# Lag, block sums and reload buffers of the second norm in a conv/pool decoder layer on eight cores

## Chip, cores and metric

The kernel runs on the 8 cores of one Trainium2 chip. Each core takes one of the 8 prompt sequences (2048 tokens) and 16 of the 128 sample sequences (128 tokens), with its own copy of the weights, and no core talks to another. The metric is the device time of the slowest core, in microseconds (us); lower is better. TensorE (matmul) is called PE here, VectorE is DVE, ScalarE is ACT, GpSimd is POOL, and SyncE (which issues most DMAs) is SP.

## What is computed

```python
h = rmsnorm(x, g_pre_mix)
p = h @ w_in                        # xv | b | c | u | gates
ya, conv_new = short_gated_conv(xv, bg, cg, conv_buf, w_conv)
ya = ya @ w_out_conv
yb, pool_new = multiscale_pool(u, pool_buf, start_pos, w_pool_group, pool_scale)
merged = gates[..., :D_MODEL] * ya + gates[..., D_MODEL:] * yb
x = x + rmsnorm(merged @ w_o, g_post_mix)
h2 = rmsnorm(x, g_pre_mlp)
f = jnp.square(jax.nn.relu(h2 @ w_up)) @ w_down
x = x + rmsnorm(f, g_post_mlp)
```

D_MODEL is 1024, D_FF is 4096, and x is float32. The matmuls run in bfloat16.

## The kernel before

A core has 17 tiles of 128 tokens: tiles 0 to 7 are half 0 of the sequence, tiles 8 to 15 half 1, and tile 16 holds the sample tokens. One big SBUF array, `AR`, is laid out by hand in byte offsets, so that buffers of later stages lie where those of earlier stages have ended. The helper class `Prog` keeps one list of instructions for each engine in the order in which the program calls them, finds dependences by overlapping bytes, and turns them into semaphore waits. An engine therefore runs its own list strictly in order, and a wait holds up all that stands behind it on that engine. The work is a list `steps`; `at_step(s, ...)` puts weight loads (issued by POOL) ahead of step s.

**Mixer.** Phase A (`a_unit`) makes the convolution branch, phase B (`phase_b`: `u_unit`, `m_unit`) the pooling branch and the gates, for half 0 and then for half 1 with the sample tokens. `phase_b(1)` ends at step `n_b`. Its last six steps are the units `m_unit` of channel blocks 6 and 7, and have no pooling work.

**Mixer tiles.** Each tile goes through three functions. `s_mm(i)` is 16 matmuls with w_o into one of four pairs of PSUM banks. `s_b1(i)` is the first norm: ACT squares and sums the pair (`sq_mix`), takes a square root, DVE takes the reciprocal and writes the scaled product (`mixn`, which frees the banks), and POOL adds the residual x in place (`x1`). `s_b2(i)` is the second norm: SP stores x1 to HBM (`x1store`), ACT squares it (`sq_x1`) and takes the root, DVE takes the reciprocal and writes `hn`, SP reloads the raw x of tile i + 3 (`load_xr`) into the buffer just left, and SP issues a DMA transpose of `hn` into the token columns of the MLP's input. Tiles 0 to 7 are spread over phase A of half 1. Tiles 8 to 16 run as one block of nine steps (`tiles2`), in the order `s_mm(i)`, `s_b2(i - 1)`, `s_b1(i)`, with three residual buffers in turn.

**MLP.** Each half is one level of a Strassen-Winograd scheme. `h_sums` makes four sums of quarters of the tokens' matrix (DVE, 128x2048 bfloat16 each), and `up_sums` four sums of weight blocks for one of 8 column blocks (DVE, 128x1024 each). `up_step(half, p)` has seven groups of 8 matmuls, three for column block p - 1 (`up_old` parts 6, 7, 4) and four for block p (`up_new` parts 1, 5, 2, 3), with DVE and ACT work between them, and calls `up_sums` for block p + 1. Half 1 also has the sample tokens in each step (`up_sample`). In half 0, step 0, `s_b2(16)` and `up_sums(0, 0)` stand ahead of all the rest. The down projection is `d0` to `d6`. `d5` and `d6` finish the output tiles: they need x1 again (`load_xl`), which goes through two buffers (`XL`). Tile t's buffer is used again for tile t + 2, whose load is issued once tile t has left it. In `d6` each tile has `gp0`, a reciprocal (L1256) and two `yl` on DVE, and two output stores on SP. Half 1 follows half 0 at once.

L139, L143, L156, L159, L169 are the lines in `Prog`'s helpers for matmul, transpose on PE, activation, tensor_tensor and scalar_tensor_tensor, so the rows are told apart by shape and time. L129 is the helper for DMAs.

Of the kernel before, what the change touches and what calls it, by code (L numbers as in the profile page):

```python
# [300 lines left out]
def build_program():  # L301
# [41 lines left out]
    with stack:  # L343
# [120 lines left out]
        XR_.append([arv(76992 + i * 4096, F32, [D]) for i in range(3)])  # L464
# [314 lines left out]
        def s_buf(i):  # L779
            v = 0 if i < 8 else 1  # L780
            return (XR_[v][i % 3], arv(MT_[v][i % 2], F32, [D]), arv(MT_[v][i % 2], BF16, [D]),
                    HN_[v][i % len(HN_[v])])

        def load_xr(i):
            P.dma("sp", s_buf(i)[0], xsrc(i), "xr%d" % (i % 3), name="xreload")
# [25 lines left out]
        def s_b2(i):  # L811
            x1, mt, mtj, hn = s_buf(i)
            x1_store[i] = P.dma("sp", x1_d[i, :, :], x1, "x1s%d" % (i % 3), name="x1store")
# [4 lines left out]
            if i + 3 < NT and (i >= 8 or i + 3 < 8):  # L818
                load_xr(i + 3)
# [33 lines left out]

        def b_last():
# [28 lines left out]
        XL = [arv(4096 + i * 4096, F32, [D]) for i in range(2)]  # L883
# [19 lines left out]
        def h_sums(half):  # L903
            t1, t2, t3, t4 = (ts_at(half, i) for i in range(4))
            P.tt("dve", t1, hq(half, 1), hq(half, 0), ALU.subtract, name="hs")
            P.tt("dve", t2, hq(half, 3), t1, ALU.subtract, name="hs")
            P.tt("dve", t3, hq(half, 3), hq(half, 1), ALU.subtract, name="hs")
            P.tt("dve", t4, hq(half, 2), t2, ALU.subtract, name="hs")
# [126 lines left out]
        def up_step(half, p, extra=()):  # L1035
# [97 lines left out]
        def d0(half):  # L1133
# [4 lines left out]
            for i in (0, 1) if half == 0 else (SMP, 9):  # L1138
                load_xl(i)
# [43 lines left out]
        def d3(half):  # L1183
# [17 lines left out]
            if half == 1:  # L1201
# [41 lines left out]
        def d6(half):  # L1243
            tl = HT[half]
            for i in range(4):
# [3 lines left out]
                xl = XL[t % 2]  # L1249
# [10 lines left out]
                if i < 2:  # L1260
                    load_xl(tl[6 + i])
# [167 lines left out]
```

How the kernel before makes its waits and increments, by code:

```python
    def emit(self, stack):  # L180
# [33 lines left out]
                            continue  # L214
                        key = d.eng
                        val = d.wait_val
                        assert val is not None, (d.name, op.name)
                    if waited.get(key, 0) >= val:
                        continue
                    if need.get(key, 0) < val:
                        need[key] = val
                for key, val in need.items():
                    waited[key] = val
                    eng.wait_ge(sems[key], val)
                    nwait += 1
                if op.fn is not None:
                    ins = op.fn(eng)
                    if op.dma is not None:
                        ins.then_inc(sems[("dma", op.dma[0])], 16)
                    elif op.signal:
                        ins.then_inc(sems[e], 1)
        return nwait
```

## Time and profile before

| | before |
|---|---|
| median of 3 runs | 1017.28 us (1015.13 to 1017.82) |
| the profiled execution | 1024.65 us |
| its span on the slowest core, core 6 | 1023.6 us |
| spans of the other cores | 1008.0 to 1019.2 us |
| mean granted clock of core 6, cores 0 to 7 | 0.958; 0.953 to 0.966 |
| PE busy | 941.8 us (92%) |
| DVE busy | 638.2 us (62%) |
| ACT busy | 361.0 us (35%) |
| POOL busy | 200.1 us (20%) |

The profiled execution was 7.4 us above the median of the runs. Times in rows are microseconds from the first instruction of core 6's span. A timeline row has start, duration, engine, line, operation and operands (output<-input), shapes and count, and in brackets the engine's idle time before it and what ended it; a row of several instructions gives the time from the first start to the last end. The duration of an instruction is from its start to its end, waits inside it included. PEclk is the share of full clock that the throttle granted.

### The profile page before, as it was taken

The page shows a single profiled execution, that of the slowest core. Times are in us where ns is not written, and L with a number is a line of the kernel's source. Part 1 is how long each engine was busy: PE and PEld are TensorE (multiplying, and loading weights), DVE is VectorE, ACT ScalarE, POOL GpSimd, SP SyncE. Part 2 cuts the span into 40 slices and gives each one's busy share as a digit, 9 for nine tenths or more (in the row PEclk, how much of TensorE's full clock was granted, in tenths as well). Part 3 has the DMA queues.
Part 4 walks back from the last instruction along what each step waited for, and adds up shares of the span by engine and source line. Part 5 has one row for each costly group of instructions (what it writes and reads, how often), then busy time and mean ns, then how long its engine had stood idle before and what let it go on. Part 6 is the DMA issues. An engine that isn't in the chain of part 4 may idle for free.

```text
span 1023.6 us, 15629 instructions; the slowest of 8 cores (1008.0 to 1023.6 us)
## 1 busy us (share of the span) xinstructions
PE 941.8 (92%) x5078; PEld 456.8 (45%) x5078; DVE 638.2 (62%) x960; ACT 361.0 (35%) x723; POOL 200.1 (20%) x203
## 2 busy tenths in 40 slices
PE   6899999999999999999961699999997899999996
PEld 4554444444455455455420244444443355544442
DVE  2567766763766666776336677658374767556186
ACT  2343432322444443233333455520133455520222
POOL 5520000000122110000133124230021243240021
PEclk7999999999999999999996799889998899999999
DMA  9699953523667653312386747594347539068027
GB/s 180 158 251 180 182 115 62 89 43 75 148 137 140 124 84 52 63 33 109 68 196 178 124 81 122 86 194 75 55 133 204 117 69 163 4 113 134 1 74 255
DMA packets 50575, 119.48 MB, mean 117 GB/s; under 512 B 21952, under 2 KB 22208, under 8 KB 50240
## 3 DMA queue, kind: packets, MB, share of 16 engines
q0 software_dynamic: 17712, 65.54, 39.6%
q1 hardware_dynamic: 32496, 52.64, 17.3%
q8 instruction: 43, 0.70, 0.3%
q14 instruction: 36, 0.29, 0.1%
q10 hardware_dynamic: 288, 0.30, 0.1%
HBM read 160.53 MB, written 19.01 MB: 175 GB/s over the span
## 4 chain that ended last, share of the span: by engine, by line
PE 72%; DVE 9%; DMA 6%; issue 5%; POOL 4%; ACT 4%; DVEq 0%; SPq 0%; ACTq 0%; POOLq 0%
PE PS L139 72%; DVE AR L169 4%; DVE AR L159 4%; ACT AR L156 3%; DMA AR<-x_d 3%; POOL AR L159 3%; DMA AR<-x_p 2%; DMA AR<-w_a 1%; DMA AR<-w_o 1%; POOL AR L164 1%; DVE STAT L427 1%; ACT STAT L156 0%; PE PS L143 0%; DVEq L224 0%; DVE AR L164 0%
## 5 line engine op out<-in xcount | busy, mean ns | idle before, releaser
L139 PE MATMUL PS<-AR 128*128 128x512 bf16 (+1 forms) x4920 | 927.0, 352 | 56.0 <-DVE AR L159 34.3
L139 PEld LDWEIGHTS PS<-AR 128*128 128x128 bf16 x4920 | 445.6, 100 | 532.2 <-issue 102.8
L156 ACT ACTIVATE AR<-PS 128x512 f32<-128x512 f32 (+3 forms) x266 | 158.6, 601 | 357.2 <-PE PS L139 315.4
L159 DVE TENSOR_TENSOR AR<-AR 128x1024 bf16<-128x1024 bf16 (+10 forms) x268 | 236.8, 903 | 70.9 <-PE PS L139 28.8
L159 DVE TENSOR_TENSOR AR<-PS,AR 128x512 f32<-128x512 f32 (+1 forms) x249 | 159.4, 649 | 154.6 <-PE PS L139 142.8
L159 POOL TENSOR_TENSOR AR<-AR 128x512 bf16<-128x512 f32 (+1 forms) x66 | 113.4, 1726 | 436.5 <-DVE AR L169 254.5
L156 ACT ACTIVATE AR<-AR 128x1024 bf16<-128x1024 f32 (+3 forms) x131 | 95.3, 739 | 115.2 <-DVE AR L159 54.7
L169 DVE SCALAR_TENSOR_TENSOR AR<-AR,CS 128x512 f32<-128x512 f32 (+1 forms) x80 | 58.3, 729 | 40.0 <-ACT AR L156 20.0
L156 ACT ACTIVATE AR<-PS,CS 128x512 f32<-128x512 f32 (+1 forms) x80 | 48.9, 621 | 76.8 <-PE PS L139 69.1
L169 DVE SCALAR_TENSOR_TENSOR AR<-AR 128x512 bf16<-128x512 f32 (+4 forms) x100 | 60.4, 629 | 3.9
L156 ACT ACTIVATE AR<-AR,CS 128x512 f32<-128x512 f32 (+1 forms) x40 | 26.3, 658 | 94.3 <-DVE AR L159 94.3
L169 DVE SCALAR_TENSOR_TENSOR AR<-AR,STAT 128x1024 bf16<-128x1024 f32 (+2 forms) x42 | 46.3, 1119 | 20.1 <-DMA AR<-x_d 16.4
L427 DVE RECIPROCAL STAT<-STAT 128x1 f32<-128x1 f32 x60 | 9.5, 158 | 65.1 <-ACT STAT L156 64.7
L129 POOL DMA_DIRECT2D AR<-w_up x32 | 17.7, 556 | 99.5 <-PE PS L139 99.2
L129 POOL DMA_DIRECT2D AR<-w_m x16 | 8.7, 544 | 139.3 <-PE PS L139 139.1
L129 POOL DMA_DIRECT2D AR<-w_a x32 | 17.6, 571 | 63.4 <-PE PS L139 57.8
L159 DVE TENSOR_TENSOR AR<-PS,CS 128x1024 bf16<-128x1024 bf16 x17 | 20.7, 1217 | 14.5 <-PE PS L143 14.5
L169 DVE SCALAR_TENSOR_TENSOR AR<-PS,CS,AR 128x512 f32<-128x512 f32 (+1 forms) x40 | 26.4, 661 | 0.0
L143 PE MATMUL PS<-IDB,AR 128*128 128x128 bf16 x136 | 11.6, 235 | 13.7 <-POOL AR L164 11.5
L169 DVE SCALAR_TENSOR_TENSOR AR<-PS,STAT,AR 128x1024 f32<-128x1024 f32 x17 | 21.8, 1284 | 2.2 <-DVE STAT L427 0.9
L164 POOL TENSOR_SCALAR AR<-AR,STAT 128x1024 bf16<-128x1024 f32 x7 | 19.9, 2848 | 15.8 <-ACT AR L156 10.6
L156 ACT ACTIVATE STAT<-STAT,CS 128x1 f32<-128x1 f32 x60 | 17.7, 294 | 5.7 <-ACT AR L156 0.4
(36 smaller groups left out, 96.4 us busy)
## 6 DMA issues: line engine op xcount, KB each, us to landing
AR<-x_p SPq DMA_DIRECT2D x32, 512.0 KB, 8.4
AR<-w_dn POOLq DMA_DIRECT2D x32, 512.0 KB, 16.0
AR<-w_m POOLq DMA_DIRECT2D x16, 768.0 KB, 10.0
AR<-w_up POOLq DMA_DIRECT2D x16, 768.0 KB, 8.9
x_d<-AR SPq DMA_DIRECT2D x17, 512.0 KB, 3.4
AR<-x_d SPq DMA_DIRECT2D x17, 512.0 KB, 4.9
AR<-w_a POOLq DMA_DIRECT2D x24, 256.0 KB, 11.0
AR<-w_a POOLq DMA_DIRECT2D x8, 768.0 KB, 9.4
```

The source lines that it names most:

```text
L129: op = self.add(q, lambda e: e.dma_start(out=out, in_=in_, **kw), reads=[in_], writes=[out], name=name, dma=(semkey, cnt))
L139: return self.add("pe", lambda e: e.matmul(out, lhsT, rhs, start=start, stop=stop, **kw), reads=[lhsT, rhs], writes=[out], signal=sig, nam ...
L143: return self.add("pe", lambda e: e.transpose(out, in_, ident), reads=[in_, ident], writes=[out], signal=signal, name="tr")
L156: return self.add("act", lambda e: e.activation(out, in_, func, **kw), reads=rd, writes=wr, name=name)
L159: return self.add(eng, lambda e: e.tensor_tensor(out, in0, in1, op), reads=[in0, in1], writes=[out], name=name)
L164: return self.add(eng, lambda e: e.tensor_scalar(out, in0, s1, s2, op0), reads=rd, writes=[out], name=name)
L169: return self.add(eng, lambda e: e.scalar_tensor_tensor(out, in0, scalar, in1, op0, op1), reads=rd, writes=[out], name=name)
L427: P.add("dve", lambda e: e.reciprocal(ss, ss), reads=[ss], writes=[ss], name="rstd")
```

## The change

The reloads of x for tiles 8 to 16 get six buffers in place of three. Those of tiles 8 to 12 are issued seven steps ahead of the end of phase B (with the state outputs, `b_last`), that of tile 13 at the first tile's step, and tile i + 6 follows in `s_b2(i)`. In `tiles2` the order becomes `s_mm(i)`, `s_b1(i)`, `s_b2(i - 2)`; `s_b2(15)` and `s_b2(16)` go into half 0's first up step, between its groups of matmuls. The four `h_sums(0)` go behind four of the last six steps of phase B, one each. `up_sums(0, 0)` goes behind the step of tile 14. Two weight loads (`load_up`) are issued a step or two sooner. x1 of each output tile has a place of its own in `AR` or one that is long free, and is loaded at the start of `d0`, `d4` and `d5`. Two pieces of `load_dn(0, 2)` and three of `load_dn(1, 1)` are issued sooner.

```diff
-        XR_.append([arv(76992 + i * 4096, F32, [D]) for i in range(3)])
+        XR_.append([arv(b_, F32, [D]) for b_ in (143360, 147456, 76992, 81088, 85184, 55296)])
...
-            if i + 3 < NT and (i >= 8 or i + 3 < 8):
-                load_xr(i + 3)
+            nx = i + 3 if i < 8 else i + 6
+            if (i < 8 and nx < 8) or (i >= 8 and nx < NT):
+                load_xr(nx)
...
+        def after(s, fn):
+            f = steps[s]["f"]
+            steps[s]["f"] = lambda: (f(), fn())
+
+        def b_tail():
+            b_last()
+            for t in range(8, 13):
+                load_xr(t)
+        after(n_b - 7, b_tail)
...
-        XL = [arv(4096 + i * 4096, F32, [D]) for i in range(2)]
+        XLB = dict(enumerate((4096, 8192, 12288, 43008, 47104, 75776, 79872, 38912,
+                              8192, 43008, 47104, 75776, 79872, 34816, 38912, 67584, 4096)))
...
+        for n_, d_ in enumerate((6, 5, 3, 2)):
+            after(n_b - d_, lambda n_=n_: h_sums(0, [n_]))
...
-        def up_step(half, p, extra=()):
+        def up_step(half, p, extra=(), mid=()):
+            mid = list(mid)
...
+            if mid:
+                mid.pop(0)()
...
-            for i in (0, 1) if half == 0 else (SMP, 9):
-                load_xl(i)
+            load_xl(*((0, 1, 2) if half == 0 else (SMP, 8)))
...
         def d4(half):
+            load_xl(*((3, 4, 5, 6) if half == 0 else (9, 10, 11, 12)))
...
         def d5(half):
             tl = HT[half]
+            load_xl(*((7,) if half == 0 else (13, 14, 15)))
...
-                out_tile(half, i, t1v(half, i), XL[t % 2], ydst(t))
-                load_xl(tl[i + 2])
+                out_tile(half, i, t1v(half, i), xl_at(t), ydst(t))
...
-                if i < 2:
-                    load_xl(tl[6 + i])
...
                 if n_ == 0:
-                    b_last()
-                    for t in range(8, 11):
-                        load_xr(t)
+                    load_xr(13)
                 s_mm(i)
-                if n_ > 0:
-                    s_b2(i - 1)
                 s_b1(i)
+                if n_ > 1:
+                    s_b2(i - 2)
                 if n_ == 6:
-                    h_sums(0)
+                    up_sums(0, 0)
             step(O_KEYS, fn)
-        at_step(n_b, lambda: load_up(0, 0))
-        at_step(n_b + 2, lambda: load_up(0, 1))
+        at_step(n_b - 2, lambda: load_up(0, 0))
+        at_step(n_b + 1, lambda: load_up(0, 1))
...
-                    if half == 0 and p == 0:
-                        s_b2(NT - 1)
-                        up_sums(0, 0)
                     if p == 8:
-                        up_step(half, p, [lambda pc=pc: d_p1(half, pc) for pc in range(4)])
+                        up_step(half, p, [lambda pc=pc: d_p1(half, pc) for pc in range(4)],
+                                [lambda: None, lambda: load_dn(1, 1, (0, 1, 2))] if half == 1 else ())
+                    elif half == 0 and p == 0:
+                        up_step(half, p, mid=[lambda: s_b2(NT - 2), lambda: s_b2(NT - 1)])
```

## Rows read from the trace of the kernel before

**Rows 1.** Who waited for whom, engine PE, whole span: total, times, longest us
```profile
PE PS L139 <- DVE AR L159: 34.3, 4, 27.4
PE PS L139 <- DVE AR L169: 12.6, 4, 3.7
```
**Rows 2.** Timeline of PE, the rows that begin after an idle time
```profile
572.23 208.38 PE L139 MATMUL PS<-AR 128*128 128x512 bf16 x920 [27.35 <-DVE AR L159]
787.24 6.04 PE L139 MATMUL PS<-AR 128*128 128x128 bf16 x44 [6.62 <-DVE STAT L1256]
...
937.71 76.13 PE L139 MATMUL PS<-AR 128*128 128x512 bf16 x352 [2.23 <-DVE AR L159]
```
**Rows 3.** Busy time by stretch, core 6: PE, PEld, DVE, ACT, POOL, PEclk, DMA share, GB/s
```profile
499.00:516.00 17.00, 17.00 (x80) 7.64 (x78) 4.57 (x8) 7.47 (x14) 5.75 (x4) 1.00 0.40 107
...
570.00:575.00 5.00, 2.77 (x7) 1.05 (x8) 4.62 (x8) 0.60 (x1) 0.00 (x0) 0.50 0.97 129
585.00:590.00 5.00, 5.00 (x21) 2.14 (x20) 4.79 (x8) 2.88 (x6) 2.02 (x2) 0.84 0.42 80
```
**Rows 4.** Timelines of ACT, DVE and POOL around tiles 8 to 10 of the block
```profile
499.12 1.02 ACT L156 ACTIVATE AR<-PS 128x1024 bf16<-128x1024 f32 x1 [3.70 <-PE PS L139]
503.95 2.34 POOL L159 TENSOR_TENSOR AR<-AR 128x1024 f32<-128x1024 f32 x1 [19.50 <-DVE AR L169]
506.38 1.06 ACT L156 ACTIVATE AR<-AR 128x1024 bf16<-128x1024 f32 x1 [4.48 <-POOL AR L159]
508.43 1.28 DVE L169 SCALAR_TENSOR_TENSOR AR<-AR,STAT 128x1024 bf16<-128x1024 f32 x1 [0.24 <-DVE STAT L427]
509.93 1.28 DVE L169 SCALAR_TENSOR_TENSOR AR<-PS,STAT,AR 128x1024 f32<-128x1024 f32 x1
511.42 2.36 POOL L159 TENSOR_TENSOR AR<-AR 128x1024 f32<-128x1024 f32 x1 [5.13 <-DVE AR L169]
```
**Rows 5.** Timelines of DVE and POOL where instructions of both meet
```profile
268.88 2.35 POOL L159 TENSOR_TENSOR AR<-AR 128x1024 f32<-128x1024 f32 x1 [11.31 <-DVE AR L169]
269.04 0.69 DVE L159 TENSOR_TENSOR AR<-PS,AR 128x512 f32<-128x512 f32 x1 [0.31 <-PE PS L139]
547.86 6.76 DVE L159 TENSOR_TENSOR AR<-AR 128x2048 bf16<-128x2048 bf16 x4
548.15 3.12 POOL L159 TENSOR_TENSOR AR<-AR 128x1024 f32<-128x1024 f32 x1 [5.00 <-DVE AR L169]
992.13 2.35 POOL L159 TENSOR_TENSOR AR<-AR 128x1024 f32<-128x1024 f32 x1 [4.78 <-DMA AR<-x_d]
993.28 2.27 DVE L169 SCALAR_TENSOR_TENSOR AR<-AR,STAT 128x1024 f32<-128x1024 f32 x1
```
**Rows 6.** DMA issues, 480 to 620 us: count, KB each, median us to landing
```profile
AR<-w_up POOLq DMA_DIRECT2D x7, 768.0 KB, 8.9
```
**Rows 7.** Timeline of DVE: one set of `up_sums`, beside no POOL add
```profile
586.21 3.53 DVE L159 TENSOR_TENSOR AR<-AR 128x1024 bf16<-128x1024 bf16 x4
```
**Rows 8.** Who waited for whom, engine DVE, whole span
```profile
DVE AR L169 <- DMA AR<-x_d: 16.4, 6, 8.9
DVE AR L159 <- DMA AR<-w_dn: 9.6, 4, 2.8
```
**Rows 9.** Timeline of DVE, end of half 0's `d6`
```profile
784.97 1.42 DVE L169 SCALAR_TENSOR_TENSOR AR<-AR,STAT 128x512 f32<-128x512 f32 x2 [8.95 <-DMA AR<-x_d]
787.91 1.41 DVE L169 SCALAR_TENSOR_TENSOR AR<-AR,STAT 128x512 f32<-128x512 f32 x2 [0.86 <-DMA AR<-x_d]
791.91 2.05 DVE L169 SCALAR_TENSOR_TENSOR AR<-AR,STAT 128x512 f32<-128x512 f32 x2 [1.91 <-DMA AR<-x_d]
```
**Rows 10.** Timelines of ACT and DVE, the last output tile
```profile
1013.94 0.60 ACT L156 ACTIVATE AR<-PS 128x512 bf16<-128x512 f32 x1 [2.38 <-PE PS L139]
1019.80 1.42 DVE L169 SCALAR_TENSOR_TENSOR AR<-AR,STAT 128x512 f32<-128x512 f32 x2 [1.71 <-DMA AR<-x_d]
```
**Rows 11.** Busy time by stretch, core 6, mixer part of half 1
```profile
260.00:500.00 240.00, 240.00 (x1440) 122.20 (x1439) 159.40 (x283) 92.59 (x212) 25.20 (x23) 1.00 0.48 97
```

More of the change, by code:

```diff
@@ L780, in s_buf @@
             v = 0 if i < 8 else 1
-            return (XR_[v][i % 3], arv(MT_[v][i % 2], F32, [D]), arv(MT_[v][i % 2], BF16, [D]),
+            return (XR_[v][i % 3 if i < 8 else (i - 8) % 6], arv(MT_[v][i % 2], F32, [D]), arv(MT_[v][i % 2], BF16, [D]),
                     HN_[v][i % len(HN_[v])])
         def load_xr(i):
-            P.dma("sp", s_buf(i)[0], xsrc(i), "xr%d" % (i % 3), name="xreload")
+            P.dma("sp", s_buf(i)[0], xsrc(i), "xr%d" % (i % 6), name="xreload")
         s_bank = {}
@@ L812, in s_b2 @@
             x1, mt, mtj, hn = s_buf(i)
-            x1_store[i] = P.dma("sp", x1_d[i, :, :], x1, "x1s%d" % (i % 3), name="x1store")
+            x1_store[i] = P.dma("sp", x1_d[i, :, :], x1, "x1s%d" % (i % 6), name="x1store")
             ss = stat()
@@ L901, in build_program, with h_sums @@
         T_1, T_2, T_3, T_4 = range(4)
-        def h_sums(half):
+        def h_sums(half, which=range(4)):
             t1, t2, t3, t4 = (ts_at(half, i) for i in range(4))
[L905 to L908, printed above, removed]
+            for o_, a_, b_ in [((t1, hq(half, 1), hq(half, 0)), (t2, hq(half, 3), t1),
+                                (t3, hq(half, 3), hq(half, 1)), (t4, hq(half, 2), t2))[i] for i in which]:
+                P.tt("dve", o_, a_, b_, ALU.subtract, name="hs")
+        for n_, d_ in enumerate((6, 5, 3, 2)):
+            after(n_b - d_, lambda n_=n_: h_sums(0, [n_]))
         def up_raw(half, b, i):
@@ L1051, in up_step @@
                 fill.pop(0)()
+            if mid:
+                mid.pop(0)()
             if o is not None:
@@ L1077, in load_dn, with xl_at, load_xl @@
                 P.dma("pool", bq(half, q, 4 * pc, 4), w_dn[q, pc], "dn%d_%d" % (q, pc), name="wload")
-        def load_xl(i):
-            P.dma("sp", XL[i % 2], x1_d[i, :, :], "xl%d" % (i % 2), name="x1load", deps=[x1_store[i]])
+        def xl_at(i):
+            return arv(XLB[i], F32, [D])
+        def load_xl(*ts):
+            for i in ts:
+                P.dma("sp", xl_at(i), x1_d[i, :, :], "xl%d" % (i % 8 if i < 16 else 8), name="x1load", deps=[x1_store[i]])
         def d_mm(bk, lhs, i, rhs, us, start, stop, sig):
@@ L1212, in d3 @@
                 b_sum(half, 2, 2, 0, ALU.subtract)
-                out_tile(half, 0, SMT, XL[0], ydst(SMP))
-                load_xl(HT[half][0])
+                out_tile(half, 0, SMT, xl_at(SMP), ydst(SMP))
         def d4(half):
+            load_xl(*((3, 4, 5, 6) if half == 0 else (9, 10, 11, 12)))
             for pc in range(4):
@@ L1248, in d6 @@
                 t = tl[4 + i]
-                xl = XL[t % 2]
+                xl = xl_at(t)
                 s0, s1 = dn[("s0", i)], stat()
@@ L1295, in build_program @@
                         at_step(s_, lambda: load_dn(0, 0))
+                    if p == 6:
+                        at_step(s_, lambda: load_dn(0, 2, (0, 1)))
                     if p == 7:
-                        at_step(s_, lambda: load_dn(0, 2))
+                        at_step(s_, lambda: load_dn(0, 2, (2, 3)))
                     if p == 8:
@@ L1313, in build_program @@
                     else:
-                        at_step(s_, lambda: (load_dn(1, 1), load_dn(1, 3)))
+                        at_step(s_, lambda: (load_dn(1, 1, (3,)), load_dn(1, 3)))
                 if n_ == 4 and half == 0:
```

## The prediction

> **What bounds the kernel now.** I read the waits of PE first, because PE is busy 941.8 of 1023.6 us. PE loses 34.3 us to DVE tensor_tensors, 27.4 of it at one point, and 12.6 us in four waits of about one tile each [rows 1]. The timeline of PE places them. It stands from 544.9 to 572.23, then 6.62 us ahead of 787.24 (and 4.75 more by 800) and 2.23 ahead of 937.71 [rows 2]. So three places are worth looking at, and the end of the program is a fourth.
>
> At the first place, the block of tiles 8 to 16, the products are not what takes time. ACT starts on tile 8's pair at 499.12 [rows 4], and 80 matmuls (five tiles) fill 499 to 516.2 without a gap [rows 3], so a tile's product is 3.44 us. Nine tiles need 31 us, yet the up projection goes on only at 572.23. One cycle shows why: POOL adds x1 for 2.34 us, then ACT squares it (506.38, 1.06 us), then DVE writes `hn` (508.43) and only behind it `mixn` of the next tile (509.93), which the next POOL add waits for (511.42) [rows 4]. From 503.95 to 511.42 is 7.5 us, and it repeats. Work of two tiles is strung into one chain, because `s_b2(i - 1)` stands ahead of `s_b1(i)` on ACT and DVE.
>
> **Part A, the lag of two tiles.** With `s_b1(i)` first and `s_b2(i - 2)` behind, nothing waits for POOL's last add. Each engine's own load per tile is then PE 3.44, ACT about 3.1 (from 506.38 to 508.43 there is a square, its root and DVE's reciprocal; 1.55 of it is ACT's, twice a tile), DVE 2.9 (two of 1.28 and two reciprocals), POOL 2.35. PE would set the pace, but for one thing. `hn` reads two operands in the SBUF, and so does POOL's add, and until now they never ran together. Where such a pair does meet, they take turns. The add from 992.13 to 994.48 left the DVE instruction of 993.28 at 2.27 us instead of 1.28, and at 547.86 POOL's add took 3.12 and four `h_sums` 6.76. A DVE instruction with one operand in the PSUM ran inside an add at its plain 0.69 (269.04) [rows 5]. So `hn` and the add are taken in turn, 1.2 + 2.35 = 3.55 us a tile, a little over PE's 3.44.
>
> Order of time, worked from 499.0:
> - PE: tile 16's product ends at 499.0 + 8 x 3.44 = 526.5.
> - POOL: x1(8) ends at 506.3; the two issues of `load_up(0, 1)`, now ahead of x1(9), take 1.1; x1(9) ends at 509.8. Then five turns of 3.55: x1(14) ends at 527.5.
> - `up_sums(0, 0)`, 3.53 us [rows 7], two-operand too, to 531.1. Then `mixn`, `hn` and x1 of tile 15 to 536.3, and those of tile 16 to 540.0.
> - The rest of tile 16 stands ahead of the next sums: ACT 1.5, DVE's `hn` 1.5, `up_sums(0, 1)` 3.5, two `C11` and two `rsq` 2.6, the first `C12` 0.7. It ends at 549.8, and PE, which has run ahead to `up_old` part 7 of step 1 with short stops, waits for it. Five groups of 8 matmuls (1.72 each) end step 1 at 558.4. Coming out of several us of stops the clock is down to 1.2 GHz for a while, as now at 570 to 575 (0.50) [rows 3]; I add 1.5: 560.
>
> Before, PE had 80 matmuls (17.2 us) left from 572.23 to the end of step 1, lost 1.4 us at 0.50 and 1.2 at 0.84 [rows 3], and ended it at 592. **Part A: 32 us less.** Bounds: if all meetings cost nothing, x1(16) ends 5 us sooner, 37; if POOL wins each meeting (rival 1), 21.
>
> What else moves here is covered. Four `h_sums` (6.76 us now, with an add taking its turn, so some 4.8 alone) go to the last six units of phase B, where DVE is under half loaded and PE has two sets of banks: nothing, and 1 to 2 us if a unit's banks were late. The reloads of tiles 14 to 16 wait on SP for the store of the tile whose buffer they take: SP has a store, a reload and a transpose per tile, and even at 8.9 us for a landing [rows 6], the longest of this stretch's kinds, x(14) issued at 511 is there by 520 and needed at 525. `load_up(0, 2)` stands behind x1(16) on POOL, is issued at 541 and lands by 550; `up_sums(0, 2)` wants it at 554. This cover is 4 us thin (rival 2).
>
> **Part B, x1 at the end of half 0.** DVE waits 16.4 us in all for x1 reloads [rows 8], and 8.95 + 0.86 + 1.91 = 11.7 of it here [rows 9]: two buffers, each reload behind the tile that frees it. The new loads of tiles 3 to 7 are issued 25 to 40 us ahead of use, into bytes whose last reader (`d3` or `d4`) is done by then. With the waits gone DVE's next limit is its own work, which has no gap there; PE's stop of 6.62 and most of the later one go. PE's clock, lowered by these stops, gives back 1.3, an estimate from the 1.4 at 0.50 in part A. **13 us less**, between 10 and 15. The six buffers cost SP nothing: the same count of loads, sooner.
>
> **Part C, three pieces of `load_dn(1, 1)` sooner.** DVE waits 9.6 us for w_dn pieces [rows 8], `C11` stands behind them on DVE and holds the banks for `d2`: PE's 2.23 [rows 2]. The pieces now go ahead of POOL's two squares and start about 6 us sooner. **2.2 less**, between 0 and 2.2.
>
> **Part D, the end.** DVE's other waits for x1, 4.6 us, lie in half 1's last tiles. ACT starts on the last product at 1013.94 (PE is done), and the last `yl` ends at 1021.2 [rows 10]. Without waits the end is 1013.9 + 1.1 for ACT (0.60, its read and root) + 0.3 for the reciprocal + 1.5 for two `yl` = 1017.0. **4.2 less**, between 2 and 4.5.
>
> **Sum.** 32 + 13 + 2.2 + 4.2 = 51.4. The profiled execution goes from 1024.65 to 973.2. It was 7.4 above the median of the runs; from the median, 1017.28 - 51.4 = 965.9, and I say 966.
>
> **Rivals.**
> 1. *POOL wins every meeting.* `mixn` starts, and POOL's add starts 1.49 us after it (509.93, 511.42); `hn` would start some 1.47 after it. If POOL is first, `hn` waits 2.35 and holds up the next `mixn`: 5.2 us a tile. For: the two starts are within 0.1. Against: from x1(9), which is late by the 1.1 us of DMA issues, `hn` is already waiting when an add ends, and then keeps first place. It costs 1.6 x 7 = 11 us: 977. By the Trainium skill, SBUF — State Buffer, section "Who interferes with whom", whoever issued first holds the port for the whole instruction; that says the same of a meeting, and not who is first here.
> 2. *Weights late.* Stores, transposes and reloads of nine tiles now share some 45 us with two `load_up`. If `load_up(0, 2)` lands 4 to 9 us beyond 550, PE waits up to 5: 971. For: a share of 0.84 to 1.0 is reached now when they meet. Against: five reloads have moved ahead of the block.
> 3. *Slower: the clock.* With the gaps gone, eight cores run dense at once. Stretches granted 0.84 and less stand in the trace now [rows 3]. From 592 to the last matmul at 1013.8, less 13.5 us of stops, PE has 408 us of work; at 0.81 it costs 94 us more, 1060, and from 220 us of it on the gain of 51 is gone. For: such stretches came behind the gap. Against: the same cores ran 240 of 240 us dense at a granted 1.00 in the mixer [rows 11]. The Trainium skill (TensorE: Matmul & The Clock Gate, section "Seeing it yourself") has a limit that takes a die to 13/16 of full clock once three of its cores run dense, while the load lasts; by it the whole rest would be at that clock and the change would lose. Rows 11 speak against it as a standing state.
> 4. *The reload waits stay*, because SP is held by some wait ahead of the new loads: 966 + 17 = 983. I see none: what stands ahead of them are stores of tiles done by then.
> 5. *Better.* No meeting costs anything, and the stretch at 0.84 behind the gap goes too: 966 - 5 - 5 = 956.
>
> **Chances.** Forecast, to within 6 us, 0.62; rival 1 0.13; rival 2 0.08; rival 3 0.03; rival 4 0.04; rival 5 0.10. The low bound takes rival 5 and the best of parts B and D: 952. The high one takes rival 1 with 6 us of a thin part B or of more clock loss: 983. About 0.3% (3 us) is what a measurement can tell. Faster 0.95, same 0.02, slower 0.03.
>
> **What would show it.** Right: POOL's adds of tiles 10 to 16 3.5 to 3.7 us apart; `hn` often 1.5 to 2.5 us long; tile 16's product ended near 527; one stop of PE of 5 to 7 us ahead of step 1's part 7; step 1 over near 560; no wait of DVE for x1; no PE stop at 787 and 937; 3.3 us from the last matmul to the last `yl`. Wrong: adds 5 us apart (rival 1), a DVE wait for w_up (rival 2), granted clock below 0.9 over a hundred us (rival 3), or DVE waits on x1 (rival 4).

## The result, and the profile after

| | before | after |
|---|---|---|
| median | 1017.55 us, 4 runs (1015.13 to 1019.12) | 971.78 us, 4 runs (971.48 to 972.59) |
| ratio | | 0.9553, 95% interval 0.9533 to 0.9573 |
| the profiled execution | 1024.65 us | 972.59 us |
| its span on the slowest core | 1023.6 us, core 6 | 971.5 us, core 3 |
| spans of the other cores | 1008.0 to 1019.2 us | 961.8 to 967.7 us |
| mean granted clock, cores 0 to 7 | 0.953 to 0.966 | 0.980 to 0.989 |
| PE busy | 941.8 us (92%) | 932.3 us (96%) |
| DVE busy | 638.2 us (62%) | 644.5 us (66%) |
| ACT busy | 361.0 us (35%) | 360.5 us (37%) |
| POOL busy | 200.1 us (20%) | 202.4 us (21%) |

The kernel is 45.8 us faster; 51.4 were forecast. Core 6 was the slowest before and core 3 is now, so the two traces are compared on core 3, whose span went from 1015.4 to 971.5 us. A few executions of the kernels below ran in a slower state, with cores of one die at a lower granted clock; all medians here leave them out, while two expectations name a median that did not (984.8 for 984.1).

The timeline of PE of the kernel after, core 3, the rows that begin after an idle time; [rows 2] is the same view of before:

```profile
533.70 6.38 PE L139 MATMUL PS<-AR 128*128 128x512 bf16 x16 [4.16 <-DVE AR L159]
541.58 5.34 PE L139 MATMUL PS<-AR 128*128 128x512 bf16 x24 [1.50 <-ACT AR L156]
553.95 197.35 PE L139 MATMUL PS<-AR 128*128 128x512 bf16 x924 [7.03 <-DVE AR L159]
752.50 1.02 PE L139 MATMUL PS<-AR 128*128 128x512 bf16 x4 [1.20 <-DVE AR L159]
754.89 210.92 PE L139 MATMUL PS<-AR 128*128 128x512 bf16 x1136 [1.38 <-DVE AR L159]
```

The same view of the kernel before, now of core 3:

```profile
519.25 3.61 PE L139 MATMUL PS<-AR 128*128 128x512 bf16 x16 [2.56 <-DVE AR L169]
533.85 5.30 PE L139 MATMUL PS<-AR 128*128 128x512 bf16 x16 [3.68 <-DVE AR L169]
...
572.84 201.10 PE L139 MATMUL PS<-AR 128*128 128x512 bf16 x920 [27.42 <-DVE AR L159]
778.34 7.32 PE L139 MATMUL PS<-AR 128*128 128x128 bf16 x44 [4.41 <-DVE STAT L1256]
788.72 1.02 PE L139 MATMUL PS<-AR 128*128 128x512 bf16 x4 [3.06 <-DVE AR L159]
791.12 135.12 PE L139 MATMUL PS<-AR 128*128 128x512 bf16 x784 [1.38 <-DVE AR L159]
928.00 76.13 PE L139 MATMUL PS<-AR 128*128 128x512 bf16 x352 [1.75 <-DVE AR L159]
```

The stop of 27.42 us, and four of 2.56 to 3.69 ahead of it (two are shown, 12.7 together), have become stops of 4.16, 1.50 and 7.03. Those of 4.41 and 3.06 have become one of 1.20, and that of 1.75 is gone. The row of four matmuls (1.02 us) is the same work in both, so the two can be laid side by side there. At it the kernel after is 788.72 - 752.50 = 36.2 us ahead. Part B's stops are 4.41 + 3.06 - 1.20 = 6.3 of it, which leaves 29.9: 27.4 for part A's stops (27.42 + 12.7 - 12.69) and 2.5 for the clock behind the stops of both parts. The last matmul ends at 1004.13 before and at 965.81 after, 38.3 ahead: 2.1 for part C (its stop was 1.75). The spans differ by 43.9: 5.6 for part D.

The granted clock was not the same on all cores before. Busy time by stretch in the kernel before, cores 6 and 3:

```profile
640.00:655.00 15.00, 15.00 (x59) 6.26 (x58) 10.85 (x16) 7.08 (x12) 3.55 (x4) 0.81 0.43 76
```

```profile
640.00:655.00 15.00, 15.00 (x71) 6.82 (x70) 12.24 (x20) 8.05 (x14) 5.42 (x7) 1.00 0.35 60
```

All eight cores have 0.81 to 0.85 from 585 to 590. Only cores 4 to 7 have it again from 640 to 655, and cores 6 and 7 once more from 670 to 685. The same 920 matmuls took 208.38 us on core 6 [rows 2] and 201.10 on core 3. In the profiled execution of the kernel after, no core has such a stretch from 560 to 960 us, but for core 3 behind its stop ahead of 752.50.

Who waited for whom, DVE and then PE of the kernel after, core 3, whole span (total, times, longest us). In the whole view for DVE there is no row for x_d, where core 3 of before has 16.0 us in six waits and core 6 had 16.4 [rows 8]:

```profile
DVE AR L159 <- DMA AR<-w_dn: 6.2, 3, 2.3
...
PE PS L139 <- DVE AR L159: 14.2, 5, 7.0
```

The block of tiles 8 to 16 in the kernel after, core 3, timelines of ACT, of POOL and then of DVE:

```profile
500.34 1.02 ACT L156 ACTIVATE AR<-PS 128x1024 bf16<-128x1024 f32 x1 [3.70 <-PE PS L139]
...
508.68 4.75 POOL L159 TENSOR_TENSOR AR<-AR 128x1024 f32<-128x1024 f32 x2
516.12 2.41 POOL L159 TENSOR_TENSOR AR<-AR 128x1024 f32<-128x1024 f32 x1 [2.69 <-DVE STAT L427]
521.46 6.58 POOL L159 TENSOR_TENSOR AR<-AR 128x1024 f32<-128x1024 f32 x2 [2.94 <-ACT AR L156]
528.61 2.35 POOL L159 TENSOR_TENSOR AR<-AR 128x1024 f32<-128x1024 f32 x1 [0.56 <-DVE STAT L427]
541.59 2.34 POOL L159 TENSOR_TENSOR AR<-AR 128x1024 f32<-128x1024 f32 x1 [2.75 <-DVE STAT L427]
...
516.15 3.47 DVE L169 SCALAR_TENSOR_TENSOR AR<-AR,STAT 128x1024 bf16<-128x1024 f32 x1
521.25 1.28 DVE L169 SCALAR_TENSOR_TENSOR AR<-AR,STAT 128x1024 bf16<-128x1024 f32 x1
528.64 3.40 DVE L169 SCALAR_TENSOR_TENSOR AR<-AR,STAT 128x1024 bf16<-128x1024 f32 x1
541.56 3.45 DVE L169 SCALAR_TENSOR_TENSOR AR<-AR,STAT 128x1024 bf16<-128x1024 f32 x1
```

The chain of [rows 4] is broken: x1(9) starts at 508.68 and x1(14) at 528.61, which is 4.0 us a tile, where it was 7.5. x1(16) ends at 543.9. The four `hn` shown are either 1.28 or 3.4 to 3.5 us long. Five of the block's nine are long, one took 1.66 and three 1.28, and it is the same five on all eight cores. All `hn` of the program stand together in a view of instructions grouped by shape (busy us, mean ns), here of the kernel before and then of the kernel after:

```profile
L169 DVE SCALAR_TENSOR_TENSOR AR<-AR,STAT 128x1024 bf16<-128x1024 f32 x17 | 21.8, 1284 | 2.5 <-DVE STAT L427 1.5
```

```profile
L169 DVE SCALAR_TENSOR_TENSOR AR<-AR,STAT 128x1024 bf16<-128x1024 f32 x17 | 33.0, 1938 | 2.5 <-DVE STAT L427 1.5
```

It is the same work at 11.2 us more: time in which DVE stands beside POOL's adds.

The end of the kernel after, timelines of PE, ACT and DVE, which answers to [rows 10]:

```profile
963.71 2.11 PE L139 MATMUL PS<-AR 128*128 128x512 bf16 x9
965.91 0.60 ACT L156 ACTIVATE AR<-PS 128x512 bf16<-128x512 f32 x1 [2.38 <-PE PS L139]
967.57 1.41 DVE L169 SCALAR_TENSOR_TENSOR AR<-AR,STAT 128x512 f32<-128x512 f32 x2
```

From the last matmul (965.8) to the end of the last `yl` (968.98) is 3.2 us.

### The profile page after: what moved, and what is told of

Same layout as the page of the kernel before. It is cut to its first block, busy times and chain, and to the rows that moved or that the text cites. A ratio compares the mean times of both kernels' runs of the same rounds, so it can differ in the third digit from the quotient of the medians.

```text
span 971.5 us, 15639 instructions; the slowest of 8 cores (961.8 to 971.5 us)
## 1 busy us (share of the span) xinstructions
PE 932.3 (96%) x5078; PEld 453.1 (47%) x5078; DVE 644.5 (66%) x960; ACT 360.5 (37%) x723; POOL 202.4 (21%) x203
## 4 chain that ended last, share of the span: by engine, by line
PE 82%; DVE 7%; issue 5%; POOL 2%; DMA 2%; ACT 2%; DVEq 0%; ACTq 0%; POOLq 0%
PE PS L139 81%; DVE AR L159 3%; DVE AR L169 3%; ACT AR L156 1%; DMA AR<-w_o 1%; POOL AR L164 1%; DMA AR<-x_p 1%; POOL AR L159 1%; POOL AR L129 0%; PE PS L143 0%; DVEq L224 0%; DVE STAT L427 0%; DVE AR L164 0%; ACT L156 0%; DVE FAC L498 0%
## 5 line engine op out<-in xcount | busy, mean ns | idle before, releaser
L139 PE MATMUL PS<-AR 128*128 128x512 bf16 (+1 forms) x4920 | 916.6, 349 | 20.1 <-DVE AR L159 14.2
L169 DVE SCALAR_TENSOR_TENSOR AR<-AR,STAT 128x1024 bf16<-128x1024 f32 (+2 forms) x42 | 55.8, 1345 | 5.0 <-DVE STAT L427 2.2
L129 POOL DMA_DIRECT2D AR<-w_up x32 | 17.8, 560 | 89.8 <-PE PS L139 89.5
L129 POOL DMA_DIRECT2D AR<-w_a x32 | 17.9, 584 | 63.9 <-PE PS L139 57.8
L159 DVE TENSOR_TENSOR AR<-PS,CS 128x1024 bf16<-128x1024 bf16 x17 | 20.7, 1219 | 13.3 <-PE PS L143 13.3
L164 POOL TENSOR_SCALAR AR<-AR,STAT 128x1024 bf16<-128x1024 f32 x7 | 19.9, 2849 | 12.9 <-DVE STAT L427 12.7
L143 PE MATMUL PS<-IDB,AR 128*128 128x128 bf16 x136 | 11.6, 234 | 11.2 <-POOL AR L164 9.2
```

The costliest lines, as they stand in the source:

```text
L129: op = self.add(q, lambda e: e.dma_start(out=out, in_=in_, **kw), reads=[in_], writes=[out], name=name, dma=(semkey, cnt))
L139: return self.add("pe", lambda e: e.matmul(out, lhsT, rhs, start=start, stop=stop, **kw), reads=[lhsT, rhs], writes=[out], signal=sig, nam ...
L143: return self.add("pe", lambda e: e.transpose(out, in_, ident), reads=[in_, ident], writes=[out], signal=signal, name="tr")
L159: return self.add(eng, lambda e: e.tensor_tensor(out, in0, in1, op), reads=[in0, in1], writes=[out], name=name)
L164: return self.add(eng, lambda e: e.tensor_scalar(out, in0, s1, s2, op0), reads=rd, writes=[out], name=name)
L169: return self.add(eng, lambda e: e.scalar_tensor_tensor(out, in0, scalar, in1, op0, op1), reads=rd, writes=[out], name=name)
```

## The experiments

Each changes the kernel after. The kernel before was run beside them, in three groups, with medians of 1019.0, 1017.1 and 1019.6 us; beside the kernel after it had 1017.55. A difference is therefore given by the medians and, in brackets, by the ratios (difference of the ratios x 1017.55). The intervals of the ratios are 2 to 7 us wide on each side, so differences below about 3 us are not told apart by times.

**A lag of one tile, the other parts kept.**

```diff
                 s_mm(i)
+                if n_ > 0:
+                    s_b2(i - 1)
                 s_b1(i)
-                if n_ > 1:
-                    s_b2(i - 2)
...
-                        up_step(half, p, mid=[lambda: s_b2(NT - 2), lambda: s_b2(NT - 1)])
+                        up_step(half, p, mid=[lambda: s_b2(NT - 1)])
```

> The changed kernel with the second norm one tile behind the first again, and ahead of it (s_b2(i - 1), then s_b1(i)); all else stays. Theory (the lag is what breaks the chain of POOL's add, the second square, hn, mixn): the adds stand 7.3 us apart again, x1 of tile 16 ends near 562 to 566, the first C12 some 20 us later than in the changed kernel, and the time is 992, 988 to 997. Rival (the sooner sums and the six reload buffers took most of the block's gain, the order little): under 980.

Measured: 991.42 us, ratio 0.9729 (0.9712 to 0.9746), 19.6 us more than the kernel after (17.9). POOL's timeline of this kernel, two adds in the block:

```profile
511.14 2.34 POOL L159 TENSOR_TENSOR AR<-AR 128x1024 f32<-128x1024 f32 x1 [3.97 <-DVE AR L169]
518.36 2.35 POOL L159 TENSOR_TENSOR AR<-AR 128x1024 f32<-128x1024 f32 x1 [4.89 <-DVE AR L169]
```

The adds are 7.2 us apart again, so the chain of [rows 4] is what the order of `s_b1` and `s_b2` makes, and nothing else of the change breaks it.

**The token and weight sums late, the lag kept.**

```diff
-        for n_, d_ in enumerate((6, 5, 3, 2)):
-            after(n_b - d_, lambda n_=n_: h_sums(0, [n_]))
...
                 if n_ == 6:
-                    up_sums(0, 0)
+                    h_sums(0)
...
+                        up_sums(0, 0)
```

> The changed kernel with the four h_sums behind tile 14's step again and the first up_sums at the start of the up projection. Theory (both then stand on DVE ahead of the first products that PE can't do without, and h_sums also delay the norms of tiles 15 and 16): 6 to 10 us slower, 978 to 982. Rival (the lag leaves DVE room for them): within 2 us of the changed kernel, 970 to 974.

Measured: 980.76 us, ratio 0.9624 (0.9605 to 0.9643), 9.0 us more (7.2). PE's timeline of this kernel:

```profile
550.47 10.79 PE L139 MATMUL PS<-AR 128*128 128x512 bf16 x40 [22.68 <-DVE AR L159]
```

PE cannot run ahead into the up steps, because their sums come last on DVE. With the lag alone a stop of 22.68 us would still stand there.

**Two x1 buffers at the end, the rest kept.** `XL` has two buffers in turn again, and tile t + 2 is loaded once tile t has left its buffer.

```diff
-            return arv(XLB[i], F32, [D])
+            return arv(4096 + (i % 2) * 4096, F32, [D])
...
                 out_tile(half, i, t1v(half, i), xl_at(t), ydst(t))
+                load_xl(tl[i + 2])
```

> The changed kernel with two x1 buffers for the output tiles again, each load issued as before behind the tile that frees its buffer. Theory (parts B and D of the forecast): DVE waits 16 us again for x1, 12 of it at the end of half 0 and 4 to 5 at the end of the program, and the time is 983 to 989. Rival (only the waits at the end of the program reach the time, those of half 0 are caught up by PE): 975 to 978.

Measured: 986.72 us, ratio 0.9682 (0.9665 to 0.9699), 14.9 us more (13.1). Waits of DVE over the whole span, and PE's timeline:

```profile
DVE AR L169 <- DMA AR<-x_d: 15.3, 6, 5.3
...
748.53 6.20 PE L139 MATMUL PS<-AR 128*128 128x128 bf16 x44 [2.97 <-DVE STAT L1278]
758.95 1.07 PE L139 MATMUL PS<-AR 128*128 128x512 bf16 x4 [4.22 <-DVE AR L159]
```

The waits of [rows 8] are back, six of them as before, and with them PE's two stops.

**`load_dn(1, 1)` whole in `d0` again.**

```diff
-                        up_step(half, p, [lambda pc=pc: d_p1(half, pc) for pc in range(4)],
-                                [lambda: None, lambda: load_dn(1, 1, (0, 1, 2))] if half == 1 else ())
+                        up_step(half, p, [lambda pc=pc: d_p1(half, pc) for pc in range(4)])
...
-                        at_step(s_, lambda: (load_dn(1, 1, (3,)), load_dn(1, 3)))
+                        at_step(s_, lambda: (load_dn(1, 1), load_dn(1, 3)))
```

> The changed kernel with all four pieces of load_dn(1, 1) issued in d0 again. Theory (part C of the forecast): PE stops about 2 us ahead of half 1's d2, and the time is 973.5 to 974.5. Rival (no core waits there any more, since the slowest cores differ): 971 to 972.5.

Measured: 974.22 us, ratio 0.9553 (0.9496 to 0.961), 2.4 us more by the medians and nothing by the ratios. The time alone says nothing here; PE's timeline does:

```profile
891.92 76.13 PE L139 MATMUL PS<-AR 128*128 128x512 bf16 x352 [2.13 <-DVE AR L159]
```

The stop ahead of these 352 matmuls, 2.23 in [rows 2], is back on the core shown. The 2.4 us are not this stop alone: in the same execution all eight cores had 0.81 to 0.86 of the clock from 565 to 570 us, cores 4 to 7 until 580, which the profiled execution of the kernel after does not show and this edit, in half 1, cannot reach.

**Three reload buffers with the lag.**

```diff
-        XR_.append([arv(b_, F32, [D]) for b_ in (143360, 147456, 76992, 81088, 85184, 55296)])
+        XR_.append([arv(b_, F32, [D]) for b_ in (143360, 147456, 76992)])
...
-            nx = i + 3 if i < 8 else i + 6
+            nx = i + 3
```

> The changed kernel with three reload buffers for tiles 8 to 16: tiles 8 to 10 loaded ahead, tile i + 3 in s_b2(i). Theory (a loop of three tiles: hn 1.3, landing 4.4 to 6, add 2.35, square and root 1.5, hn, so 3.5 to 4.5 us a tile, which is less than the 5.1 that a blocked hn makes of it): small, 972 to 977, and POOL waits for x_p. Rival (the reloads, now behind hn of the tile two back, set the pace of the block): 982 to 990.

Measured: 992.44 us, ratio 0.9728 (0.9666 to 0.9791), 20.7 us more (17.8). That is above the range of the rival, whose mechanism it is. Waits of POOL, from 480 to 620 us:

```profile
POOL AR L159 <- DMA AR<-x_p: 21.4, 5, 5.3
```

With three buffers the reload of tile i + 3 stands behind the second norm of tile i, which now comes two tiles later, and five of the adds wait for their residual. The kernel before, with three buffers and a lag of one, has no such wait on any core. So the six buffers would save nothing there, yet all that the lag gives hangs on them.

**`hn` with one operand in the SBUF.** The weight row `g_pre_mlp` is copied into a pair of PSUM banks that is held for the block. The products and the first up steps have three pairs left.

```diff
+                    gp.append(bank2())
+                    held.update((gp[0], gp[0] + 1))
+                    P.copy("act", pair(gp[0]), GPL, name="gpl")
...
-            P.stt("dve", hn, x1, ss, GPL, ALU.mult, ALU.mult, name="hn")
+            if gp:
+                P.stt("dve", hn, pair(gp[0]), ss, x1, ALU.mult, ALU.mult, name="hn")
+            else:
+                P.stt("dve", hn, x1, ss, GPL, ALU.mult, ALU.mult, name="hn")
```

> The changed kernel with g_pre_mlp copied once by ACT into a pair of PSUM banks held for the block of tiles 8 to 16, so that hn has one operand in the SBUF and POOL's add has no partner to take turns with; the products then have three pairs of banks. Theory (hn and the add exclude each other while both read two operands in the SBUF): each hn of the block takes 1.28 us, none 3.4; the adds follow the products 3.5 us apart; x1 of tile 16 ends 6 to 10 us sooner, and the time is 964, 961 to 967. Rival (the long hn are hidden by PE's lead of four tiles or made up later): 970 to 973. A third (three pairs of banks hold PE up): above 973.

Measured: 984.14 us, ratio 0.9664 (0.9639 to 0.9688), 12.4 us *more* (11.3). The spans of the profiled execution fall into two groups: cores 0, 1, 3, 6 and 7 took 955.1 to 963.6 us, less than any core of the kernel after but core 6, and cores 2, 4 and 5 took 973.3 to 979.5. Core 3 is of the first group. Its `hn` of this block grouped by shape, POOL's adds of tiles 12 to 14 and 16, and PE's last stop:

```profile
L169 DVE SCALAR_TENSOR_TENSOR AR<-PS,STAT,AR 128x1024 bf16<-128x1024 f32 x9 | 11.6, 1283 | 1.1 <-DVE STAT L427 0.4
...
515.81 2.36 POOL L159 TENSOR_TENSOR AR<-AR 128x1024 f32<-128x1024 f32 x1 [0.79 <-DVE STAT L427]
519.11 2.36 POOL L159 TENSOR_TENSOR AR<-AR 128x1024 f32<-128x1024 f32 x1 [0.93 <-DVE STAT L427]
522.56 2.35 POOL L159 TENSOR_TENSOR AR<-AR 128x1024 f32<-128x1024 f32 x1 [1.09 <-DVE STAT L427]
532.51 2.35 POOL L159 TENSOR_TENSOR AR<-AR 128x1024 f32<-128x1024 f32 x1 [0.70 <-DVE AR L169]
...
545.87 74.37 PE L139 MATMUL PS<-AR 128*128 128x512 bf16 x336 [3.80 <-DVE AR L159]
```

No `hn` is stretched, the adds of tiles 12 to 14 are 3.3 to 3.5 us apart, and PE's last stop ends at 545.87 in place of 553.95. (Its block began 1.9 us sooner; the other 6.2 are the gain.) That much came as expected. The time lies where the third theory, too few banks, would have it, but that is not the cause: with the same three pairs and no transposes, further down, this kernel took 963.54. Core 2 is of the other group; its stretch, one transpose on SP's queue, and the DMA view from 480 to 620 us (count, KB each, median us to landing):

```profile
530.00:550.00 20.00, 14.96 (x69) 6.33 (x68) 11.66 (x18) 11.02 (x21) 5.72 (x9) 1.00 1.17 111
...
532.90 18.87 SPq L828 DMA_TRANSPOSE AR<-AR  x1
...
AR<-w_up POOLq DMA_DIRECT2D x7, 768.0 KB, 28.4
```

The packets' times add up to 1.17 of what the DMA engines have, and they move only 111 GB/s (the jam, from here on); on core 3 the same 20 us show 1.07 at 238 GB/s. One transpose keeps SP for 18.87 us and weights land after 28.4 us in place of 8.1 on core 3. There DVE waits 27.0 us for w_up. Late weights alone do not mark a slow core, though: they landed after 17.3 and 14.4 us on cores 1 and 6 of the fast group, and after 10.4 and 9.5 on cores 4 and 5. Nor does one transpose of 10 us, which cores 0, 1 and 3 have too (10.2 to 10.9). Core 4 shows another wait (ACT's waits from 480 to 620 us, then PE's timeline):

```profile
ACT AR L156 <- DMA AR<-AR: 25.7, 4, 17.9
...
561.15 3.57 PE L139 MATMUL PS<-AR 128*128 128x512 bf16 x8 [18.08 <-DVE AR L169]
```

ACT's `sq_x1` writes an `hn` buffer whose transpose is still under way (it keeps SP for 18.71 us), and PE stands for 18.08 us behind it.

**The jam: which transfers?** Two tries first moved work out of its way. In one, `load_up(0, 2)` is issued with tile 12's step, ahead of POOL's later adds:

```diff
+        at_step(n_b + 4, lambda: load_up(0, 2))
```

> The kernel of the run e3_hn_psum, with load_up(0, 2) issued three steps sooner, ahead of tile 12's add and not behind tile 16's. In that run six cores took 955 to 964 us, and one to three others 973 to 985, where stores, transposes and two load_up issued back to back met and some landed 20 to 39 us late. Theory (the two loads together behind the last add, on top of five transposes in flight, make the jam): no core with a landing of w_up or a transpose over 20 us behind 530, the slowest core at 962 to 966. Rival (any load beside the denser stores and transposes can jam): again one or more cores 10 us and more above the others, 975 to 985.

Measured: 984.91 us, ratio 0.9665 (0.9598 to 0.9731), no better. Core 5, the slowest, by stretch:

```profile
540.00:550.00 10.00, 5.04 (x16) 1.83 (x16) 1.45 (x2) 1.59 (x5) 0.00 (x0) 0.83 1.35 50
```

The other also has `up_sums(0, 0)` two tiles sooner and the second norms of tiles 15 and 16 later, the last of them in up step 1:

```diff
-                if n_ == 6:
+                if n_ == 4:
                     up_sums(0, 0)
...
-                        up_step(half, p, mid=[lambda: s_b2(NT - 2), lambda: (s_b2(NT - 1), drop(gp[0]), drop(gp[0] + 1))])
+                        up_step(half, p, mid=[lambda: None, lambda: s_b2(NT - 2)])
+                    elif half == 0 and p == 1:
+                        up_step(half, p, mid=[lambda: (s_b2(NT - 1), drop(gp[0]), drop(gp[0] + 1))])
```

> The kernel of the run e5_psum_load2 with up_sums(0, 0) behind tile 12's step and not tile 14's, and the second norms of tiles 15 and 16 one place later each (between later groups of step 0, and in step 1), so that the sums, C11 and rsq of block 0 don't stand behind hn of tile 16. Theory (PE's last stop of 3.8 us is the chain of tile 16 ahead of the first C12): 2 to 4 us less than e5_psum_load2, 958 to 963. Rival (the DVE is full there, and the stop only moves to step 1): the same as e5_psum_load2 within 1.5 us.

Measured: 979.86 us, ratio 0.9609 (0.9555 to 0.9663), where 958 to 963 was expected. The best cores of its profiled execution took 958 to 962 us, the slowest 980.3.

So the transposes of tiles 8 to 16 were left out, once with `hn` reading the PSUM and once with `hn` as it is. Half 1's MLP input is then never written, and its output is wrong.

```diff
-            P.add("sp", lambda e: e.dma_start_transpose(out=dst, in_=hn), reads=[hn], writes=[dst], name="xpose",
-                  dma=(key, cnt))
+            if i < 8:
+                P.add("sp", lambda e: e.dma_start_transpose(out=dst, in_=hn), reads=[hn], writes=[dst], name="xpose",
+                      dma=(key, cnt))
```

> The kernel after with the factor of hn (g_pre_mlp) in a held pair of PSUM banks, so that hn has one operand in the SBUF, and without the DMA transposes of tiles 8 to 16 (half 1's MLP input is left unwritten, so half 1's output is not the reference's). With the transposes this kernel's slowest core took 984.8 us and its undisturbed ones 955 to 964. Theory (the jam is the transposes meeting w_up loads and x1 stores): no core is left above 966, all eight lie within 955 to 966, slowest about 962. Rival (stores and weight loads jam by themselves once the block is dense): one to three cores stay at 973 to 985, DVE waits for w_up 10 us or more there.

Measured: 963.54 us, ratio 0.9456 (0.9434 to 0.9478), spans 955.5 to 963.9 on all eight cores.

> The kernel after, without the DMA transposes of tiles 8 to 16 (half 1's output is not the reference's), hn as it is. Theory (in the kernel after the transposes cost next to nothing, its block is paced by hn and POOL's add): 968 to 972, at most 3 us under 971.8. Rival (they already hold back its slowest core): 962 to 967. hn stays at 3.4 us where it meets an add.

Measured: 969.84 us, ratio 0.9529 (0.9497 to 0.956), spans 961.9 to 967.5. The packets of all queues from 480 to 620 us, first of the kernel after, then of the PSUM kernel without transposes with its w_up loads:

```profile
DMA packets 14778, 21.68 MB, mean 155 GB/s; under 512 B 10082, under 2 KB 10082, under 8 KB 14767
```

```profile
DMA packets 5524, 20.21 MB, mean 144 GB/s; under 512 B 615, under 2 KB 615, under 8 KB 5512
...
AR<-w_up POOLq DMA_DIRECT2D x8, 768.0 KB, 8.7
```

Nine transposes make two of three packets in this stretch, all under 512 B. Without them no core is slow and w_up lands in 8.7 us, with the same stores, reloads and weight loads meeting at the same density. The jam needs the transposes; which step of them makes it, these runs do not tell, since SP and ACT's waits for `hn` buffers are relieved too. These two runs also price the meetings of `hn` and the add: 969.84 - 963.54 = 6.3 us, and the intervals lie apart. What else differs (one pair of banks held, one copy on ACT) is extra on the side of the faster one.

**More room for the transposes.** Six `hn` buffers and five reload buffers, with `hn` reading the PSUM, and without:

```diff
-        XR_.append([arv(b_, F32, [D]) for b_ in (143360, 147456, 76992, 81088, 85184, 55296)])
+        XR_.append([arv(b_, F32, [D]) for b_ in (143360, 147456, 76992, 81088, 85184)])
...
-        HN_.append([arv(b_, BF16, [D]) for b_ in (89280, 91328, 72896, 74944)])
+        HN_.append([arv(b_, BF16, [D]) for b_ in (89280, 91328, 72896, 74944, 55296, 57344)])
...
-            nx = i + 3 if i < 8 else i + 6
+            nx = i + 3 if i < 8 else i + 5
```

> The kernel after with the factor of hn in a held PSUM pair, six hn buffers in place of four and five x reload buffers in place of six (x of tile i + 5 loaded in the second norm of tile i). Theory (of the jam the 15 to 18 us in which ACT waits for a transpose to leave the hn buffer are what stops PE, and two more buffers hide a transpose of up to 24 us): slowest core 966 to 974 in place of 984.8, no ACT wait for a transpose above 5 us. Rival (the jam stops weights as well): still 978 to 986, with DVE waits for w_up or POOL waits for x_p on the slow cores.

Measured: 993.32 us, ratio 0.9741 (0.9713 to 0.9769): worse than with four, and above both expectations. In its profiled execution (989.08 us) one transpose still holds ACT for 15.3 us on core 3, DVE waits 12.4 us for w_up on core 4, and POOL waits for x_p on every core, 1.9 to 7.6 us.

> The kernel after with six hn buffers and five x reload buffers, hn as it is. Theory: ACT waits for transposes only 0.7 to 3.3 us on any core there, so 969 to 972.5, no difference that can be told from 971.8. Rival (five reload buffers are too few, x of tile 13 comes late): 975 or more, with POOL waits for x_p.

Measured: 972.44 us, ratio 0.9562 (0.9521 to 0.9604), as expected not to be told from the kernel after. Its profiled execution was the longest of the three that count, 978.99 us; waits of ACT and PE's timeline there on the slowest core, core 4:

```profile
ACT AR L156 <- DMA AR<-AR: 8.3, 1, 8.3
...
593.48 165.24 PE L139 MATMUL PS<-AR 128*128 128x512 bf16 x765 [5.18 <-ACT AR L156]
```

ACT waits 8.3 us for a transpose on this core and 3.9 on core 5, and on the other six not at all; with four buffers it waited 0.7 to 3.3 us on every core. Why six buffers made the denser kernel worse is not shown. The four buffers may also have held back how many transposes are under way, and five reload buffers came with the six. No variant here that computes the whole result beats the kernel after.

## Why the prediction was right, and where it was off

**Part A, 32 forecast, 29.9 found on core 3 (clock included).** The mechanism held: undoing the lag alone costs 19.6 us, and undoing the order of the sums alone 9.0 (17.9 and 7.2 by the ratios). The step that was off is "from x1(9) ... `hn` is already waiting when an add ends, and then keeps first place", and with it 3.55 us a tile. The measured pace is 4.0 us. Set against ACT's square of tile 8, which starts 1.2 us later on this core than in [rows 4], x1(16) was due at 541.2 and ended at 543.9, and PE's last stop was due to end at 551.0 and ended at 553.95. The adds were not evenly 3.5 to 3.7 us apart either: 4.0 on the mean of five, and 7.9 from tile 14 to tile 15, where `up_sums(0, 0)` stands. Only one `hn` of nine took 1.5 to 2.5 us. `hn` kept first place only where it had begun 0.2 us sooner (521.25 against 521.46). Where both began within 0.04 us, in either order, `hn` took 3.4 to 3.5 us (516.15 against 516.12; 541.56 against 541.59). So rival 1's way of meeting was the rule, in five of the block's nine tiles. Its price was not: after each lost meeting POOL gets its next `mixn` late, starts late, and the next meeting can be won. With all else in this chain it came to 2.7 us over the forecast, and not 11. The whole of the meetings, forecast at 5 us, is worth 6.3.

The Trainium skill (SBUF — State Buffer, "Who interferes with whom") says: "Issue order, not op shape, decides who blocks." The trace agrees where the starts are 0.2 us apart; where they are 0.03 apart, the starts in the trace don't tell who was first.

**Part B, 13 forecast, 6.3 on core 3.** Right in kind: no wait for x1 is left, and most of the stops went. The term was mis-sized in three ways. It was read from core 6, whose stops here (6.62 and 4.75) are together the longest of the eight cores; core 3 lost 4.41, 3.06 and 1.38. Of those, 1.20 and 1.38 stayed, on core 6 as well (1.18 and 1.38), where the forecast let all of it go. And its 1.3 for the clock stands, on core 3, in part A's number.

**Part C, 2.2 forecast, 2.1 on core 3.** PE's stop of 1.75 us there is gone, and the undone part brings back one of 2.13.

**Part D, 4.2 forecast, 5.6 on core 3.** From the last matmul to the last `yl` is 3.2 us; 3.3 were forecast (its terms add up to 1016.8 and not 1017.0, which changes nothing). Core 3 had more to lose than core 6: its three DVE waits at the end were 3.68, 0.46 and 1.81 us. Taken together, B and D were forecast at 17.2, and undoing both cost 14.9 by the medians (13.1 by the ratios).

**The sum.** Core 3's parts are 29.9 + 6.3 + 2.1 + 5.6 = 43.9, and the medians differ by 45.8, where 51.4 were forecast. The miss is in the sizes, 2.1 in part A and 6.7 in part B on this core, less 1.4 that part D gave beyond its forecast. The four single undoings come to 19.6 + 9.0 + 14.9 + 2.4 = 45.9 by the medians, and to 38.2 by the ratios. The gain is these four parts; how it is shared out is known to some 2 us each.

**Where luck helped.** For the profiled execution the forecast was 973.2, and it took 972.59. That nearness is partly luck. From slowest core to slowest core the gain is 1023.6 - 971.5 = 52.1, and 8.2 of it is what core 6 had above core 3 before the change. 208.38 - 201.10 = 7.3 us of that is the low clock on core 6, mostly in stretches that the prediction did not read, and whose end no term of its sum stands for. They made up for what part B gave less. That the profiled execution stood above the median, by 7.4 us, was taken as something that the change would leave in place; it did not.

**The rivals.** Rival 2, weights late: no DVE wait for w_up shows, and w_up lands in 8.7 us, in 8.9 in [rows 6]. (The prediction calls these 8.9 us the longest landing of the stretch; the same view has 9.6 for the smaller w_up pieces and 16.5 for w_dn. Nothing hung on it, since the x reloads on SP's queue landed in 4.2 in the kernel after.) Its mechanism is nearer than it looked, though. It is what the kernel with `hn` in the PSUM runs into, and in the kernel after one transpose on each core already keeps SP for 5.3 to 7.3 us, where the others take 1.2 to 3.4.

Rival 3, the clock: the granted clock rose to 0.980 to 0.989, with PE busy for 96% of the span on core 3. The Trainium skill (TensorE: Matmul & The Clock Gate, "Seeing it yourself") would have the whole rest at 13/16 of full clock; the trace does not agree. The low stretch of this part of the trace stands behind PE's stop, 0.52 from 555 to 560 us on core 3, and is over by 560. Stretches at 0.81 did stand in the kernel before, and not only behind the gap as the prediction says (640 to 655 on cores 4 to 7). They are absent from the profiled execution of the kernel after and present in that of the kernel with `load_dn(1, 1)` late, which has the same block, so what brings them stays open.

Rival 4, reload waits: none at the end of the program. With three buffers in the mixer they would have taken the whole of the lag's gain.

Rival 5, better: the five cores on which the meetings were gone and the jam did not come took 955.1 to 963.6 us, so its mechanism is real, and its price is the jam. The stretch at 0.84 behind the gap, its second term, is gone on every core of the profiled execution.

What stays open: what in the chip makes a few transposes last 15 to 20 us when they meet weight loads, and why it strikes some cores and not others in one execution. The runs show only that it goes with the transposes and that it is worse when the block is denser.

## What to carry to other kernels

When each tile goes through two chains on the same engines, put the first chain of the next tile ahead of the second of the last one, and check at once what the longer lag does to buffers: here three reload buffers would have taken back all that the lag gives. Price an edit on every core, not on the slowest alone: what makes one core the slowest of one execution, here longer stops and a lower clock, need not be there on the others. Before making a dense block denser, look at what its small-packet transfers do on all cores; the time is that of the worst core, and seven faster ones don't help.

## What the hardware showed that was not expected

- A two-operand DVE instruction and a POOL add that begin within 0.04 us of each other: DVE's took 3.39 to 3.47 us in place of 1.28 in all five cases, on each of the eight cores. With one operand in the PSUM the nine took 1.28 (mean 1283 ns, core 3) beside the same adds.
- DMA transposes of 128x1024 bfloat16 kept SP's queue for 1.2 to 3.4 us in the kernel after, but for one of 5.3 to 7.3 on each of its eight cores, and for 18.87 and 18.71 on cores 2 and 4 of the kernel with `hn` in the PSUM. On core 2 there, and on core 5 of the try with `load_up(0, 2)` sooner, the packets' times came to 1.17 and 1.35 of what the DMA engines have in such a stretch, with 111 and 50 GB/s moved.
- The granted clock had stretches of 0.81 to 0.85 lasting 5 to 20 us, with PE busy throughout, on all cores or on one die only, in some executions and not in others.
- Nine transposes (9 x 128 x 1024 x 2 bytes, 2.4 MB) account for some 9,500 packets under 512 B, next to 5,300 others that carried the remaining 19.3 MB.
